# Moving a group norm's statistic, root, scaling and parts past six softmax units

## The reference

```python
o_sb  = stick_breaking_attention(sb_q, sb_k, sb_v)     # 8 heads of 64: 512 columns ("stick")
o_mla = mla_attention(q_nope, q_rope, k_nope, k_rope, v_mla)   # 8 heads of 64: 512 columns ("latent")
mix = jnp.concatenate([rms_norm_2(o_sb, g_grp_sb), rms_norm_2(o_mla, g_grp_mla)], axis=-1) @ w_o
```

## Time and profile before

| | |
|---|---|
| median of 3 runs | 1039.91 us (1037.68 to 1041.69) |
| the profiled execution, own time | 1044.3 us |
| its span, first to last instruction | 1042.5 us |
| PE busy, share of the span | 1001.9 us, 96% |
| DVE, ACT, POOL busy | 773.0, 610.7, 162.5 us |
| latent attention, first scores to first matmul of `o` | 747.3 to 769.4 us |

### The profile page before, as it was taken

How to read it: one execution, slowest core, us unless ns; L and a number is a source line. 1 busy time by engine, 2 the same in 40 slices (tenths; PEclk the granted TensorE clock), 3 DMA queues, 4 the chain that set the end, 5 groups by cost and what they waited for, 6 DMA issues and landing times.

```text
span 1042.5 us, 18130 instructions
## 1 busy us (share of the span) xinstructions
PE 1001.9 (96%) x7019; PEld 902.4 (87%) x7019; DVE 773.0 (74%) x1450; ACT 610.7 (59%) x1145; POOL 162.5 (16%) x88
## 2 busy tenths in 40 slices
PE   7989999999999997899999999998999999999997
PEld 6978888888899986788878889997799999999876
DVE  4888779867867858866987676676556778767786
ACT  6634557564646767646647464566546565645465
POOL 2953102212100001000121120102000000101201
PEclk9999999999999998999999999999989899999999
DMA  9572154554545440034555545422403355554521
GB/s 365 186 240 71 52 202 163 203 193 171 202 163 201 167 163 1 1 122 162 178 191 197 202 167 194 168 93 77 162 1 138 146 191 176 201 183 171 175 78 41
DMA packets 25284, 160.50 MB, mean 154 GB/s; under 512 B 2800, under 2 KB 5104, under 8 KB 7152
## 3 DMA queue, kind: packets, MB, share of 16 engines
q1 hardware_dynamic: 24912, 158.31, 42.8%
q10 hardware_dynamic: 288, 1.05, 0.3%
HBM read 157.86 MB, written 1.49 MB: 153 GB/s over the span
## 4 chain that ended last, share of the span: by engine, by line
PE 84%; DVE 10%; issue 3%; ACT 2%; POOLq 0%; DVEq 0%; POOL 0%; ACTq 0%
PE bank L767 80%; PE obank L767 3%; DVE split_lo L629 2%; PE bank L930 1%; DVE tmp L2255 1%; DVE hidden_parts L2247 1%; DVE rowmax L2808 1%; DVE tmp L2247 1%; DVE probs L2251 0%; ACT probs L1584 0%; DVE sq L2247 0%; DVE pt_lo L2247 0%; DVE x L2247 0%; DVE y L2255 0%; DVE y L2247 0%
## 5 line engine op out<-in xcount | busy, mean ns | idle before, releaser
L621 ACT ACTIVATE split_hi<-ring 128x1024 fp32r<-128x1024 f32 (+1 forms) x280 | 289.9, 1048 | 117.7 <-PE bank L767 116.5
L767 PE MATMUL bank<-act_parts,split_hi 128*128 128x256 f32 (+1 forms) x1696 | 319.5, 288 | 8.5 <-DVE act_parts L2247 3.8
L629 DVE TENSOR_TENSOR split_lo<-ring,split_hi 128x1024 fp32r<-128x1024 f32 (+1 forms) x221 | 269.7, 1229 | 34.2 <-ACT split_hi L621 33.6
L767 PEld LDWEIGHTS bank<-act_parts,split_hi 128*128 128x128 f32 x1696 | 265.1, 191 | 16.5 <-issue 11.0
L767 PE MATMUL bank<-hidden_parts,split_hi 128*128 128x512 f32 (+1 forms) x944 | 268.4, 351 | 5.6 <-DVE hidden_parts L2247 2.8
L629 POOL TENSOR_TENSOR split_lo<-ring,split_hi 128x1024 fp32r<-128x1024 f32 (+1 forms) x59 | 143.7, 2447 | 682.6 <-ACT split_hi L621 682.5
L767 PE MATMUL bank<-act_parts,split_lo 128*128 128x256 f32 x880 | 248.3, 282 | 0.0
L767 PE MATMUL bank<-hidden_parts,split_lo 128*128 128x256 f32 x752 | 210.9, 280 | 0.0
L767 PEld LDWEIGHTS bank<-hidden_parts,split_hi 128*128 128x128 f32 x944 | 165.1, 189 | 31.8 <-DVE split_lo L629 3.1
L767 PE MATMUL bank<-mlp_parts,split_hi 128*128 128x512 f32 x512 | 178.7, 391 | 1.1 <-DVE mlp_parts L2255 1.1
L767 PEld LDWEIGHTS bank<-act_parts,split_lo 128*128 128x128 f32 x880 | 167.7, 191 | 0.0
(11 more groups left out here) (286 smaller groups left out, 1234.8 us busy)
## 6 DMA issues: line engine op xcount, KB each, us to landing
ring<-in_weights SPq DMA_DIRECT2D x140, 1024.0 KB, 4.8
ring<-in_weights SPq DMA_DIRECT2D x5, 768.0 KB, 4.2
ring<-in_weights SPq DMA_DIRECT2D x3, 512.0 KB, 7.3
shifted<-conv_rows SPq DMA_DIRECT2D x9, 142.0 KB, 5.3
x<-in_x ACTq DMA_DIRECT2D x2, 512.0 KB, 6.5
y<-in_mem SPq DMA_DIRECT2D x1, 1024.0 KB, 12.2
out<-x SPq DMA_DIRECT2D x4, 256.0 KB, 2.9
consts<-in_consts SPq DMA_DIRECT2D x1, 933.0 KB, 13.8
```

Source lines behind the costliest of these rows:

```text
L621: nc.scalar.activation(split_hi[:, w % SPLIT, 0:n], src, ACT.Copy).then_inc(sem("high_parts"), 1)
L629: (nc.vector if engine == "vector" else nc.gpsimd).tensor_tensor(split_lo[:, w % SPLIT, 0:n], src, split_hi[:, w % SPLIT, 0:n].bitcast(F32 ...
L767: return nc.tensor.matmul(dst, lhsT, rhs, start=start, stop=stop)
```

## The change

The stick norm's statistic, root, scaling and parts are taken out of the six units and put behind them. The PSUM tiles `sb.stat` and `sb.bc` move to the end of the list of the units' tiles.

```diff
# psum_tiles
-        if w == 0:
+        if w == n:
             linear("sb.stat", 1)
-        if w == 3:
+        if w == n:
             linear("sb.bc", 1)
# PE
-                if w == 0:
+                if w == len(units):
                     full_stat("sb", 4)
-                if w == 3:
-                    full_bcast("sb")
                 if w == 2:
                     wait_emptied(pe, "v_up", 0)
                     wait_emptied(pe, "v_up", 1)
                 if w >= 2:
                     outputs("mla", units[w - 2], w - 2)
+            full_bcast("sb")
# ACT
             stick_squares(range(4))
-            exponentials("mla", range(2))
+            exponentials("mla")
             root("sb", 2, 512)
-            exponentials("mla", range(2, 4))
-            wait_emptied(act, "sb.bc", 0)
-            high(flat(act_hi[:, 0:4, :]), flat(mix[:, 0:4, :]), "sb.high")
-            exponentials("mla", range(4, 6))
             for tt in range(TT):
                 c = RC["mla"] + tt
                 wait_out_emptied(act, ("mla", "mla", tt, 0))
                 settle(do(flat(sq[:, 0:2, :]), otok[:, tt, 0:512], ACT.Square, accum_out=smalls[:, c:c + 1]))
                 do(smalls[:, c + 2:c + 3], smalls[:, c:c + 1], ACT.Sqrt, const("eps6"), 1.0 / 512)\
                     .then_inc(sem("mla.root"), 1)
+                if tt == 0:
+                    wait_emptied(act, "sb.bc", 0)
+                    high(flat(act_hi[:, 0:4, :]), flat(mix[:, 0:4, :]), "sb.high")
# DVE, beside the units
-                if w == 2:
+                if w == len(units):
                     invert("sb", 2)
-                if w == 3:
-                    wait_tile(dve, "sb.bc", 0)
-                    for t in range(4):
-                        last = stt(mix[:, t, :], osb[:, t, :], const("g_sb", t, 1), bank("sb.bc", 0)[:, 0:SEQ], ALU.mult, ALU.mult)
-                    last.then_inc(emptied("sb.bc", 0), 1)
-                if w == 5:
-                    dve.wait_ge(sem("sb.high"), 1)
-                    low(flat(act_lo[:, 0:4, :]), flat(mix[:, 0:4, :]), flat(act_hi[:, 0:4, :]), "o.act")
# DVE, behind the units
                 ts(otok[:, tt, 0:512], otok[:, tt, 0:512], rc[:, c:c + 1], ALU.mult).then_inc(sem("mla.o"), 1)
+                if tt == 0:
+                    wait_tile(dve, "sb.bc", 0)
+                    for t in range(4):
+                        last = stt(mix[:, t, :], osb[:, t, :], const("g_sb", t, 1), bank("sb.bc", 0)[:, 0:SEQ], ALU.mult, ALU.mult)
+                    last.then_inc(emptied("sb.bc", 0), 1)
+            dve.wait_ge(sem("sb.high"), 1)
+            low(flat(act_lo[:, 0:4, :]), flat(mix[:, 0:4, :]), flat(act_hi[:, 0:4, :]), "o.act")
```

## The result

| | before | after |
|---|---|---|
| median of 12 runs each, us | 1038.30 (1035.32 to 1041.69) | 1043.62 (1041.61 to 1046.84) |
| ratio, 95% interval | | 1.0048 [1.0033, 1.0063] |
| profiled execution: span | 1042.5 | 1042.1 |
| first latent scores, from the span's start | 747.31 | 744.88 |

What follows compares the result with a forecast made beforehand. PE was taken to bound the kernel; units gaining about 4 us against a 7.1 us chain gave +3.2 us, plus 1 us for the clock: +4.2 us on 1039.91, 1044.1 us; range +0.5 (1040.4) to +8.1 (1048.0).

Steps and rivals of the forecast that it cites:

- PE's path is all that counts, and today PE starts `o` without a wait: PE carries 84% of the chain; stick parts are ready at 766.67, before `o` starts at 769.39.
- The units, worked out anew: Retimed latent attention units: unit 2's exponentials gain 2.6 us without two table loads; outputs 5 end about 4 us earlier.
- The chain behind outputs 5: Serial DVE and ACT work through the low part takes 7.1 us; PE restarts at 772.6, 3.2 us later.
- The clock: Half clock at the start of `o`: 1 us added, giving +4.2; bounds +1.7 and +4.7 in all.
- the wait at 762.3: PE's wait for unit 4's exponentials, cited as agreeing that a long idle gap sends the clock to half rate.
- The 1048.5 us set for the profiled execution: The same 4.2 us added to the profiled execution of 1044.3 us, giving about 1048.5.
- the prediction's own signs of being wrong: PE wait under 4 us, outputs 5 later than 768, or a shift shrinking again later in `o` or its norm.
- The clock falls before the statistic ends: Rival: the moved statistic and outputs 4 and 5 double at half clock, +6.6 us, or +8.1; chance 0.30.
- PE and ACT run further ahead: Rival: exponentials of units 2 to 5 run back to back, PE restarts about 768.8, -0.6 us; chance 0.15.
- The units do not shrink: Rival: something else paces the units, outputs 5 stay at 769.6, full chain added, +7.1 us; chance 0.07.
- Bank order, DMA: In the units: the new bank rotation costs nothing, scores 5 being met over 2 us early; no DMA is moved.

Runs made afterwards that it cites:

- parts late: Kernel before, with only the products, high part and low part moved behind the units; statistic, root and broadcast left among them; ratio to before 1.0065.
- low first: Changed kernel, with DVE's low part of the stick tiles put ahead of the scaling of half 1 of the latent outputs; ratio to before 1.0038.
- No switch: Kernel before, with the stick norm's root replaced by an activation needing no other table, so two table loads between units 1 and 2 go; ratio 0.9989.
- parts between: Kernel before, with products two steps later, high part behind all exponentials and low part behind the last copy; ratio to before 0.9998.
- short statistic: Kernel before, with the stick norm's statistic cut from 16 matmuls to 4, summing one of four tiles; ratio to before 0.9966.
- folded: The kernel of parts between, with GpSimd adding the four squared tiles to one, so the statistic takes 4 matmuls; ratio to before 0.9981.
- folded in parts: The kernel of folded, with high and low parts made tile by tile and PE waiting for each in turn; ratio to before 0.9981.
- its second: The changed kernel, unaltered, timed and profiled a second time; ratio to before 1.0044.
- busy wait: Changed kernel, with 28 bf16 matmuls of 512 columns on PE inside its wait for the stick parts; ratio to before 1.0048.
- sticks first: Changed kernel, with the whole stick chain put ahead of the latent norm and the broadcast between outputs 4 and 5; ratio to before 1.0014.
- by tiles: The kernel of sticks first, with high and low parts tile by tile and first halves of three `o` tiles ahead of the `otok` transposes; ratio 1.0000.

## Why the prediction was right

**PE's path is all that counts, and today PE starts `o` without a wait.** Right; the new bracket of 6.59 us is where the time went.

**The units, worked out anew.** Right in its times: exponentials of unit 2 at 753.57 on the scale of before, measured 753.61 (+6.30); last exponentials done at 761.40, measured 761.37 with the read of the last sum, which the forecast's price has in it; outputs 5 done at 765.5, measured 765.61. Wrong in one reason: it read two loads between units 1 and 2 as what the exponentials of unit 2 waited for. In the kernel before they were covered by PE, which was held by the statistic and by half clock behind it. Since these left together with the loads, the sum came out the same; that is luck in the reason, and with the loads alone gone the same working would have given 2.6 us that were not there.

**The chain behind outputs 5.** 7.1 us forecast, 7.08 measured, and 7.09 in parts late; low first removed its 1.5 us link. PE's restart at 772.6 was measured at 772.69. This step carried the prediction.

**The clock.** This is the weak term. The chain and the units give +3.2 us, and one us was added for the clock. The reason given for it (most of the phase at full clock) speaks for the lower bound of 1.7, but the us was added toward the upper one, 4.7. Up to ple the trace has 3.34 us in all (50.51 less 47.17), so there the clock added next to nothing: 0.22 us in the 24 matmuls. That the one us brought the forecast nearer to the measured 5.0 is luck as far as the runs show. The prediction also took the wait at 762.3 as a case of a long idle gap that throttles the clock. That wait was 1.44 us, and the clock fell at +18.6, 1.8 us after PE had gone on. It is the changed kernel that shows such a gap: the clock fell 3.6 us into PE's idle time and was at 0.50 at the restart.

The rest of the 5.0 us lies most likely in the trace that the forecast started from. It had 6.9 us of half clock over its last outputs and `o` (+18.6 to +25.5). No switch, whose exponentials end at the same place to the hundredth, did not have it, and stood 2.7 us earlier at oT. From the first latent scores to the end the trace of before takes 295.19 us. The other kernels give an estimate of what it takes as a rule: for each of the eleven that are neither before nor after, the same stretch of its trace, less what its ratio says that it differs from before. That gives 291.7 to 295.6 us, 292.7 in the middle. By this estimate the trace of before is some 2.5 us long behind the first scores, and the changed kernel (297.22 and 296.97) costs 4.4 us, inside 5.0 [3.4, 6.6]. It is no measurement: how often the kernel before has that half clock was not counted.

The 1048.5 us set for the profiled execution were 1043.9. Of these 4.6 us, 2.43 are its faster unchanged first part, 0.86 the shift at ple (3.34 where 4.2 was set), and 1.31 lie behind ple (246.71 us against 248.02). So in this pair of traces the shift does shrink again, to 2.0 us at the end. That is close to the last of the prediction's own signs of being wrong, but it happens behind `o` and ple, and from ple to the end the fourteen traces scatter between 246.3 and 249.5 us.

**The rivals.** *The clock falls before the statistic ends:* no, in both traces it held until +22.4, 4.1 us behind the outputs; the moved statistic ran at full clock (1.71 us from its start to the outputs'). *PE and ACT run further ahead:* no, the maxima, copies and the first group's finish paced them as forecast. *The units do not shrink:* no, by 4 us they did. *Bank order, DMA:* between the first latent scores and ple PE's only waits are for ACT's exponentials (0.29 and 0.40 us) and for the low part (6.59).

## What to carry to other kernels

Before moving work behind a loop, write down the chain that will stand between the loop's last result and the next matmul, in the order of each engine's queue; here it was seventeen instructions long on two engines and took 7.1 us, where before PE had no wait, for 4 gained. An engine's visible stall (two table loads) is not the bound if another engine is later still: without the loads alone the exponentials ended where they had, and with the others gone too up to 2 us earlier. Judge one profile beside the scatter of runs: here the profiled execution of the kernel before was slower (1044.3 us) than every timed one of 95 (up to 1043.65). When parts must be made late, put them in front of everything that the next consumer does not need. Cutting them by tiles as well brought PE's restart forward by 2.5 us; what that is worth in the time isn't shown apart from the smaller statistic.

## What the runs showed of the hardware

Behind the 16 one-column matmuls of the statistic at the head of the units, during which PE counts as fully busy, a half-clock stretch of 3.4 us followed in four traces of four (before, no switch, parts late, parts between: from +4.9 to +5.4 on). With 4 such matmuls in the same place there was none in three of three (short statistic, folded, folded in parts). Behind the units the same 16 were followed by outputs at full clock in five traces (after and its second, busy wait, low first, sticks first), but in by tiles the clock fell at +18.4, 2.1 us behind them. So they do not bring it down everywhere, and it was not tested whether in the units it is they or the time that they take. The Trainium skill (TensorE: Matmul & The Clock Gate, "What's actually happening") says that the throttled state is the default and that activity releases the throttle. In these traces a row that shows PE as fully busy did not tell whether the clock would hold.

A table load on ACT took 1.28 us, and the next instruction started at once when its input was there (754.64 behind the load at 753.34, in the kernel before). The load was issued ahead of the semaphore wait of the instruction that needed it: in the changed kernel it ended 1.14 us ahead of the root's data. In four kernels with both loads between the units (before, short statistic, folded, folded in parts) the exponentials of unit 2 started at +8.90, right behind the second load, whether their maximum had been ready for 0.1 us (before) or for 2.5 (folded).
